# Layer 1's output projection half in split products, its weights split during the attention, and finer releases of the expert stream

## The reference

```
q, k, v = jnp.split(h @ w_in, 3, axis=-1)          # 1024 -> 3072
...                                                # rotary positions, softmax, times v
return _merge_chunks(o) @ w_out                    # the output projection, 1024 x 1024
...
x = layer_norm(DN_ALPHA * x + mix, ...)
ffn = grouped_moe(x, ...)                          # 16 experts of 1024 x 512 (gate, up) and 512 x 1024 (down)
x = layer_norm(DN_ALPHA * x + ffn, ...)
```

## Time and profile before

| what | us |
|---|---|
| three runs | 745.62, 746.95, 748.08 (median 746.95) |
| the profiled execution, its time | 747.59 |
| its span on the core | 745.8 |
| layer 1's attention on PE, first transposes to the last product | about 462 to 489 |
| layer 1's experts on PE | about 527 to 736 |

### The profile page before, as it was taken

How to read it: one execution, slowest core, us unless ns; L and a number is a source line. 1 busy time by engine, 2 the same in 40 slices (tenths; PEclk the granted TensorE clock), 3 DMA queues, 4 the chain that set the end, 5 groups by cost and what they waited for, 6 DMA issues and landing times.

```text
span 745.8 us, 9008 instructions
## 1 busy us (share of the span) xinstructions
PE 722.0 (97%) x3693; PEld 388.7 (52%) x3693; DVE 282.9 (38%) x527; ACT 201.0 (27%) x459; POOL 111.1 (15%) x91
## 2 busy tenths in 40 slices
PE   8999999999999999999899999999999999999994
PEld 5877766774344344343347887656434434434331
DVE  4385675363222121122155785636322212112214
ACT  5343689232110110110033546513210011011101
POOL 0011378312000000000043221401200000000001
PEclk9999999999999999999999999999999999999997
DMA  9999800167999999999999964016799999999992
GB/s 329 311 382 422 366 1 1 58 245 299 356 430 431 427 427 427 428 427 420 421 388 387 413 230 185 30 57 239 301 362 431 431 423 432 423 430 425 421 420 107
DMA packets 42700, 245.06 MB, mean 329 GB/s; under 512 B 5920, under 2 KB 10144, under 8 KB 29344
## 3 DMA queue, kind: packets, MB, share of 16 engines
q1 hardware_dynamic: 42656, 244.43, 81.5%
HBM read 243.37 MB, written 1.05 MB: 328 GB/s over the span
## 4 chain that ended last, share of the span: by engine, by line
PE 81%; DMA 9%; DVE 5%; ACT 2%; POOL 1%; issue 1%; SPq 0%; DVEq 0%
PE ps L861 25%; PE ps L882 13%; DMA ring<-in_w_up 8%; PE ps L781 5%; PE ps L583 4%; PE ps L585 4%; PE ps L584 4%; PE ps L846 3%; PE ps L892 3%; PE ps L674 2%; PE ps L660 2%; PE ps L699 2%; PE ps L837 1%; DMA ring<-in_w_in 1%; ACT R L1166 1%
## 5 line engine op out<-in xcount | busy, mean ns | idle before, releaser
L861 PE MATMUL ps<-ring,R 128*64 128x512 f32 x928 | 227.1, 595 | 0.4 <-DMA ring<-in_w_up 0.4
L861 PEld LDWEIGHTS ps<-ring,R 128*64 128x64 f32 x928 | 70.6, 137 | 108.8 <-issue 107.2
L882 PE MATMUL ps<-ring,R 128*64 128x512 f32 x448 | 113.4, 595 | 0.6 <-issue 0.6
L1117 ACT ACTIVATE wh<-ps,small 128x512 fp32r<-128x512 f32 x32 | 22.0, 688 | 266.2 <-PE ps L882 264.6
L1453 DVE TENSOR_TENSOR wl_r<-ring,wh 128x512 fp32r<-128x512 f32 x72 | 55.7, 791 | 42.6 <-ACT wh L1095 42.2
L882 PEld LDWEIGHTS ps<-ring,R 128*64 128x64 f32 x448 | 35.0, 137 | 67.7 <-issue 65.2
L1679 DVE SCALAR_TENSOR_TENSOR wl_r<-ps,small,wh 128x512 fp32r<-128x512 f32 x32 | 24.0, 751 | 105.3 <-ACT wh L1117 104.6
L583 PE MATMUL ps<-wh,xh_r 128*128 128x512 f32 x144 | 57.7, 400 | 1.1 <-DVE wl_r L1453 1.0
L1095 ACT CAST wh<-ring 128x512 fp32r<-128x512 f32 x72 | 44.5, 624 | 49.2 <-PE ps L585 48.2
L1668 DVE TENSOR_TENSOR R<-R,ps 128x512 f32<-128x512 f32 x16 | 17.2, 1074 | 105.6 <-PE ps L861 105.6
L585 PE MATMUL ps<-wh,xl 128*128 128x512 f32 x144 | 56.2, 391 | 0.0
(11 more groups left out here) (223 smaller groups left out, 995.4 us busy)
## 6 DMA issues: line engine op xcount, KB each, us to landing
ring<-in_w_gate SPq DMA_DIRECT2D x28, 2048.0 KB, 18.4
ring<-in_w_up SPq DMA_DIRECT2D x22, 2048.0 KB, 18.6
ring<-in_w_down SPq DMA_DIRECT2D x22, 2048.0 KB, 20.8
ring<-in_w_in SPq DMA_DIRECT2D x21, 1024.0 KB, 14.2
ring<-in_w_out SPq DMA_DIRECT2D x8, 1024.0 KB, 14.7
R<-in_w_up SPq DMA_DIRECT2D x4, 2048.0 KB, 17.8
R<-in_w_down SPq DMA_DIRECT2D x4, 2048.0 KB, 20.1
ring<-in_w_gate SPq DMA_DIRECT2D x8, 1024.0 KB, 26.1
```

Source lines behind the costliest of these rows:

```text
L861: last = mm(ps[64 * e:64 * e + 64, to, :], xe[:, j, at + 64 * e:at + 64 * e + 64], slots[e][:, j * UNIT:(j + 1) * UNIT], start=(j == 0), s ...
L882: last = mm(ps[64 * e:64 * e + 64, 2 + w, :], hT[:, k, 64 * e:64 * e + 64], slots[e][:, at:at + UNIT], start=(k == 0), stop=(k == FJ - 1))
```

## The change

Three things are changed.

First, the weight stream. In both layers blocks 11 to 16 of the experts are loaded in halves; the first halves are issued when PE has used half of the place (`HALF_FREED`, counted by `gate_part`, which now goes up six times in a layer), the second when all is free. The last two down blocks come in quarters, each with its own counter, and the last `from_hidden` uses the order (k, w) of the others and waits for quarter k, where it had taken w = 0 of a half before w = 1 of it.

Second, layer 1's output projection does steps 0 to 3 of both column halves in three fp32r products (`PIECED = [6, 4]`). The high part of the weights is cast by DVE, two chunks each in its iterations m = 3 to 6; the low part is subtracted by POOL, two chunks each behind the scaling of items 4 to 7. The groups of items 0, 1 and 2, 3 are cast by ACT (`group_hi`, behind the exponentials of items 5 and 7), and DVE subtracts where it copied. PE waits for `wo_lo` before the first step of each half.

Third, the copy of the transposed probabilities in layer 1 is shared: DVE copies one half, ACT the other (`PT_COPIES = [2, 2]`), as in layer 0.

```diff
-        PIECED = 6
-        WO_AT = [0] * 2 + [1] * 9 + [3]
-        WO = [(w, j) for w in range(2) for j in range(PIECED)]
+        PIECED = [6, 4]
+        WO_AT = [[0] * 2 + [1] * 9 + [3], [0] * 4 + [2] * 4]
+        WO = [[(w, j) for w in range(2) for j in range(PIECED[l])] for l in range(2)]
...
+        HALF_FREED = range(SLOT + 3, SLOT + 9)
+        FREED = 6
+        LASTDOWN = 6 * PAIRS - 2
...
-        PT_COPIES = [2, 1]
+        PT_COPIES = [2, 2]
...
+            def load_half_freed(n, freed):
+                l = n // (6 * PAIRS)
+                for h in range(2):
+                    for what in (("moe", n), ("moe", n + 1)):
+                        if h == 0:
+                            sp.wait_ge(main.gate_part, FREED * l + freed)
+                        else:
+                            slot_free(what)
+                        i, k = divmod(what[1] % (6 * PAIRS), 6)
+                        c = slice(2 * D * h, 2 * D * (h + 1))
+                        sp.dma_start(in_slot(what)[:, c], expert_src(l, 2 * i + k % 2, k // 2)[:, c]
+                                     ).then_inc(landing(what, h)[0], 16)
...
-                for n in range(SLOT + 3, LASTROUND):
+                for n in HALF_FREED[::2]:
+                    load_half_freed(6 * PAIRS * l + n, 4 + HALF_FREED.index(n) // 2)
+                for n in range(HALF_FREED.stop, LASTROUND):
                     load_expert(6 * PAIRS * l + n)
-                for n in range(LASTROUND, 6 * PAIRS, 2):
+                for n in range(LASTROUND, LASTDOWN, 2):
                     load_halves(6 * PAIRS * l + n)
+                load_last_down(l)
...
-                    if l == 0 and a == 0:
-                        pe.wait_ge(wo_lo, PIECED * (w + 1))
-                pieces = PIECED if l == 0 else 0
+                    if a == 0:
+                        pe.wait_ge(wo_lo, WO_BASE[l] + PIECED[l] * (w + 1))
+                pieces = PIECED[l]
...
-                                  rd.gate_part if i == 0 and w == 0 else None)
+                                  rd.gate_part, {(0, 0): (2, 4, 6), (0, 1): (4,), (1, 0): (4,)}.get((i, w), ()))
...
+                def group_hi(u):
+                    act.wait_ge(L.pv, B.pv + ITEMS[l] // 4 * (u + 1))
+                    copy(OT2_HI[u], ps[:, 6 + u % 2, :]).then_inc(L.ot_sb, 1)
...
-                    if l == 0 and m >= 2:
+                    if m >= 2:
                         copy_probs_t(m - 2)
                     exponentials(m)
...
+                    if l and m in (5, 7):
+                        group_hi(m // 2 - 2)
...
-                if l == 0 and u < 3:
+                if u < PIECED[l] // 2:
                     dve.wait_ge(L.ot_sb, B.ot_sb + 2 * u + 1)
                     tt(OT2_LO[u], ps[:, bank, :], OT2_HI[u], ALU.subtract).then_inc(L.ot_sb, 1)
...
+                    for c, (w, j) in wo_chunks(1, m + 1) if l and 3 <= m < n - 1 else []:
+                        if c == WO_BASE[1]:
+                            dve.wait_ge(L.proj, B.proj + 12)
+                        dve.wait_ge(*landing(("unit", OUT[2 + w]), j // 4))
+                        copy(WO_HI[w][j], in_slot(("unit", OUT[2 + w]))[:, j * UNIT:(j + 1) * UNIT]).then_inc(wo_hi, 1)
```

More of the change, by code:

```diff
@@ L450, in load_halves, with load_last_down @@
                                      ).then_inc(landing(what, h)[0], 16)
+            def load_half_freed(n, freed):
[10 more added lines that the diff above has]
+                                     ).then_inc(landing(what, h)[0], 16)
+            def load_last_down(l):
+                for q in range(4):
+                    for e in range(2):
+                        what = ("moe", 6 * PAIRS * l + LASTDOWN + e)
+                        if q == 0:
+                            slot_free(what)
+                        c = slice(D * q, D * (q + 1))
+                        sp.dma_start(in_slot(what)[:, c], expert_src(l, E - 2 + e, 2)[:, c]).then_inc(last_quarter(l, e, q)[0], 16)
             def load_quarters(n):
-                l, q0 = n // (6 * PAIRS), 3 * (n // (6 * PAIRS))
+                l, q0 = n // (6 * PAIRS), FREED * (n // (6 * PAIRS))
                 for q in range(4):
@@ L849, in gather, with to_hidden @@
                 last.then_inc(rd.gathered, 1)
-            def to_hidden(to, xe, at, slots, done, parts=(), second=(), part_done=None):
+            def to_hidden(to, xe, at, slots, done, parts=(), second=(), part_done=None, part_at=()):
                 for j in range(KJ):
@@ L873, in transpose_hidden, with from_hidden @@
                 last.then_inc(rd.ht, 1)
[L875 to L879, removed]
+            def from_hidden(rd, slots, half_done=None, quarters=None):
+                for k, w in ((k, w) for k in range(FJ) for w in range(2)):
+                    if half_done and (k, w) == (2, 0):
+                        last.then_inc(half_done, 1)
+                    if quarters and w == 0:
+                        for e in range(2):
+                            pe.wait_ge(*quarters(e, k))
                     for e in range(2):
@@ L937, in experts @@
                     pe.wait_ge(rd.gsum, n + 1)
-                    for e in range(2):
+                    for e in range(2 if i < PAIRS - 1 else 0):
                         pe.wait_ge(*landing(chunks[4 + e], 0))
-                        if i == 1 and in_halves(chunks[4 + e]):
+                        if i < PAIRS - 1 and in_halves(chunks[4 + e]):
                             pe.wait_ge(*landing(chunks[4 + e], 1))
@@ L970, in spare_round @@
                     pe.wait_ge(rd.ht_sb, n1)
-                    from_hidden(rd, [ring[:, 4], ring[:, 5]], [(k, w) for w in range(2) for k in range(FJ)])
+                    from_hidden(rd, [ring[:, 4], ring[:, 5]])
                     combine(rd, 0, (pe.snap(2 * i + 2 * PAIRS * rho + 1), pe.snap(2 * i + 2 * PAIRS * rho + 2)))
@@ L1279, in _ @@
                     copy_probs_t(ITEMS[0] - 1)
+                else:
+                    for m in range(ITEMS[1] - 2, ITEMS[1]):
+                        copy_probs_t(m)
                 def rows_copy(a, w):
```

38 lines of the change are left out of this document (21 added, 17 removed).

## The result

The changed kernel takes 753.56 us (median of four runs, 752.90 to 754.23), the kernel before 747.52 beside it. The ratio is 1.0071, 95% interval 1.0048 to 1.0093: slower, by 0.7%. In a second comparison on another chip it came out at 753.39 us and 1.0105 (1.0068 to 1.0141). A ratio compares all undisturbed executions of two kernels and isn't the quotient of their medians; one execution each of the kernel before (762.09 us), of `best` (827.87) and of `whole_copies` (1869.58) is left out as slow. The forecast of 748.6 was too low, and its range, which ended at 751.3, too. The profiled execution took 753.21 us with a span of 751.2, 5.4 more than the span before.

What follows compares the result with a forecast made beforehand. PE, busy for 97% of the span, was taken as the bound. Attention 6.4, products -1.8, stream -3.1 and last down product +0.2 gave +1.7 us on 747.6, 749.3; as a median 748.6 us, range 745.0 to 751.3.

Steps and rivals of the forecast that it cites:

- The stream, -3.1 us: Expert up blocks: half-block issue closes transfer gaps; PE's waits of 1.85 us in layer 0, 1.28 in layer 1 go.
- The order of the last down product, +0.1 a layer: Last down product: its first half completes one step before the end rather than two; +0.2 us over both layers.
- The products, 0.15 us a step: Layer 1's projection: three products save 0.15 us a step over float32; twelve steps behind the attention give -1.8 us.
- The chain of handoffs: Layer 1's attention: products of items 1, 3, 5 come 0.9, 3.9, 6.7 us later through ACT and DVE; end 6.4 later.
- The rival by which the handoffs cost little: Layer 1's attention: products of items 3 and 5 move half as much, 745.2 us, or not at all, 742; chance 0.15.
- The 0.8 us that PE was to wait for POOL before the two split steps: Gap before item 5's product: PE waits 0.8 us for POOL's subtractions, done at 485.6, well before 487.9.
- PE's clock stays at 1.00 in the attention: Layer 1's attention: the prediction named a clock there other than 1.00 as a sign it was wrong.
- The rival on it: PE's clock falls to 1.2 GHz in the 3.5 us gap before item 3's product: +2 us, 750.6; chance 0.18.
- the sum's +1.7: Whole kernel: all terms together add 1.7 us to the profiled execution's 747.6, giving 749.3.
- DVE and POOL hold each other up: Layer 1's attention: casts meeting POOL's scalings wait or hold them up, about +1.2 us, 749.8; chance 0.13.
- the term of +0.9: Product of item 1, layer 1's attention: two casts and a half copy, 2.07 us, replace DVE's 1.21 us copy; +0.9 us.

Runs made afterwards that it cites:

- best: Changed kernel with DVE's casts and subtractions, ACT's group casts and POOL's low parts moved in layer 1's attention; 744.69 us, ratio 0.9958 to the kernel before.
- whole_copies: Changed kernel with the third change undone: in layer 1 DVE alone copies the transposed probabilities in one piece; 754.08 us, ratio 1.0095 to the kernel before.
- stream_only: Kernel before with the changed weight stream alone, layer 1's attention and projection as before; 744.43 us against 747.96, ratio 0.9958.
- fill_gaps: Changed kernel with matmuls adding zeros before layer 1's products of items 1, 3 and 5, where PE would idle; 750.45 us, ratio 1.0028 to the kernel before.
- collect_late: Changed kernel with DVE's group subtractions one iteration later, behind the half copies of items 3 and 5; 748.79 us, ratio 1.0015 to the kernel before.
- proj_only: Changed kernel with the weight stream of the kernel before, the second and third changes kept; 762.14 us, ratio 1.0185 to the kernel before.

## Why the prediction was wrong

- *The stream, -3.1 us.* Right in mechanism, a little small. stream_only is 3.5 us below its reference by the medians. The waits of the earlier trace rows are gone, the stretches of the earlier trace rows run at 424 and 415 GB/s. Before, PE had waited for the up blocks of layer 0 three times, 2.3 us in all, and not 1.85.
- *The order of the last down product, +0.1 a layer.* In layer 1 PE waits 0.77 us for DVE where it had waited 0.44 before the last combination, so +0.3: right in sign, but three times the 0.1.
- *The products, 0.15 us a step.* Right. In layer 1 PE starts four split steps at 514.46 and the next operation at 517.31, 2.85 us; four float32 steps take 521.18 - 517.74 = 3.44 us. The stage behind the attention is 2.0 us shorter (1.8 predicted).

```profile
514.46 0.48 PE L820 MATMUL ps<-xl,R_r 128*128 128x512 f32 x1
...
517.31 0.60 PE L834 MATMUL ps<-cst,R 128*128 128x128 f32 x4
517.74 3.60 PE L817 MATMUL ps<-ring,R 128*128 128x512 f32 x8
521.18 0.29 PE L852 MATMUL ps<-small,cst 128*128 128x16 f32 x2
```

- *The chain of handoffs.* Right in mechanism. ACT's row for the chain at item 3 and DVE's:

```profile
473.79 0.58 ACT L1295 COPY R<-ps 128x512 f32<-128x512 f32 x1 [2.19 <-PE ps L710]
474.27 0.48 ACT L1203 ACTIVATE R<-ps,small 128x256 f32<-128x256 f32 x1
...
476.08 0.61 ACT L1210 CAST R_r<-ps 128x512 fp32r<-128x512 f32 x1
```

```profile
476.72 0.69 DVE L1597 TENSOR_TENSOR R_r<-ps,R_r 128x512 fp32r<-128x512 f32 x1 [1.73 <-ACT R_r L1210]
477.33 0.68 DVE L1832 COPY R<-ps 128x512 f32<-128x512 f32 x1
```

  Half copy, exponentials, group's cast, subtraction, half copy, product: 478.06 - 473.79 = 4.27 us, and 0.2 in front of it, where I had 4.66. At full clock (fill_gaps) the attention grows by 7.3 us where I had 6.4. The rival by which the handoffs cost little has fallen. The 0.8 us that PE was to wait for POOL before the two split steps didn't come; they lay off the path, as the prediction had it.
- *The step that failed is that PE's clock stays at 1.00 in the attention.* The forecast counted all of PE's work between the waits at full clock. The rival on it was there, but for one gap of 3.5 us, at one price of 2 us and with a chance of 0.18. For the waits at items 1 and 5 the prediction put nothing and gave no reason; its longest wait at full clock was the 1.33 us of the earlier trace rows, and between that and 3.5 us it had no row. The clock fell behind all three waits, that of 1.95 us too, and took 3.5 us together: the span's +5.4 exceeds the sum's +1.7 by 3.7 us. The other errors of the sum nearly cancel: the chain at full clock +0.9, the stages outside the attention -0.7. The rest of the 5.0 us between forecast and median, 1.3 us, lies outside the sum: 0.6 is the kernel before, whose median beside the changed one was 747.52 and not 746.95, and the rest is how the profiled executions and their spans lay against the medians.
- *DVE and POOL hold each other up.* This rival was true in mechanism, and the size of the cast hid it. A cast alone takes 0.38 to 0.42 us (a pair 0.75), not the 0.69 that I took from a copy out of PSUM; a pair that meets POOL's instructions takes 1.06 to 3.33. At item 1 the pair took 1.58 where I had 1.38, so the term of +0.9 came out near its 1.0 by luck, through two errors that cancel. Alone the pair would have taken 0.75, and the wait 1.1 us instead of 1.95. The 1.19 us of the earlier trace rows were an instruction with two inputs in SBUF and not a copy, so they showed that DVE is held up beside POOL, but not that a cast is. By the Trainium skill ("VectorE: DVE Perf Modes", the perf-mode tier table) an estimate for such a copy is 0.42 us; the trace of best agrees, with 0.75 us for the pair with POOL idle. By the Trainium skill ("SBUF — State Buffer", who interferes with whom) a DVE copy in its two-port mode and a POOL instruction exclude each other; the trace agrees, with 0.75 us for a pair alone against 2.67 beside POOL. In these rows DVE bears nearly all of it.

## What to carry to other kernels

Where PE is the bound, a wait that an edit brings is priced twice: its own length, and the work behind it at half clock, unless a trace of the same kernel shows a wait as long with the clock at 1.00 behind it. An instruction that waits for another engine belongs behind everything in its queue that a third engine is waiting for; here that one place was half of the attention's loss, and moving it took 5.4 us off the attention. Work that fits an engine's idle share still needs idle time at the right moment, and, for DVE's casts inside SBUF, a moment when POOL is idle: the split products saved 2.0 us behind the attention and, in the order as given, the attention that had to make room for them grew by 10.8.

## What the runs showed of the hardware

- PE's granted clock fell to 0.50 behind waits of 1.95, 3.23 and 2.91 us, and not behind waits of 2.04 us (collect_late) and 1.47 (best): the length of one wait alone didn't decide. A slow stretch made PE's work 1.3 to 2.5 us longer.
- bf16 matmuls of 512 columns in the waits kept it at 1.00 (fill_gaps, 0.23 us each).
- A DVE cast of 128x512 from SBUF to SBUF, float32 to fp32r, takes 0.38 us behind another, and up to 2.1 beside POOL's tensor instructions; the cast that was held up ended 0.3 us after POOL's instruction. A DVE copy out of PSUM beside POOL kept its 0.68 us. POOL's scaling of 1024 columns grew from 1.89 to 2.08 us at most.
- The profiled executions lay up to 3.2 us apart at layer 0's first product with v (94.2 to 97.4 us), in code that all these kernels share; in proj_only, the latest of them, the clock was 0.93 between 50 and 100 us.
